# Three modulation panels of a gap at once, each in a column group of its own, with one set of transposes

## What is computed

```
mod  = jax.nn.silu(c)     @ w_ada[i] + b_ada[i]     # c, c_ctx: 1024 values; w_ada[i]: 1024 x 6144
modc = jax.nn.silu(c_ctx) @ w_ada[i] + b_ada[i]
sh1, sc1, gt1, sh2, sc2, gt2 = jnp.split(mod[:, None, :], 6, axis=-1)
h = rmsnorm(x, g_norm1[i]) * (1 + sc1) + sh1
```

## Time and profile before

| | us |
|---|---|
| median of 3 runs | 3118.34 (3117.12 to 3120.02) |
| the profiled execution | 3123.84 |
| its span in the trace | 3121.5 |
| TensorE busy | 2756.1 (88%) |
| TensorE weight loads busy | 1632.0 (52%) |
| VectorE busy | 811.8 (26%) |
| ScalarE busy | 506.5 (16%) |
| matmuls of the panels, line 538 | 384 records |
| matmuls of the folds, line 554 | 192 records |

### The profile page before, as it was taken

One profiled execution on the slowest core, in us unless ns is written; L12 is line 12 of the kernel. 1 busy time (PEld: TensorE's weight loads), 2 busy tenths in 40 slices (PEclk: granted clock), 3 DMA queues, 4 the chain that ended last, 5 costly groups with the idle time before them and its releaser, 6 DMA issues.

```text
span 3121.5 us, 30855 instructions
## 1 busy us (share of the span) xinstructions
PE 2756.1 (88%) x13271; PEld 1632.0 (52%) x13271; DVE 811.8 (26%) x1735; ACT 506.5 (16%) x1045; POOL 50.5 (2%) x76
## 2 busy tenths in 40 slices
PE   6989999999999999999997888988999996666766
PEld 4658887677885444444443323323456884222322
DVE  2343402153522534332212010111334412000001
ACT  1340001031002012122202111011211321000001
POOL 0000000000001100000000000000200000000000
PEclk8999999989999999999998999999999998777776
DMA  9346446417447311121213999999521334999996
GB/s 311 135 173 197 157 148 245 159 50 247 151 146 188 101 54 43 40 80 45 76 67 121 421 421 421 418 422 392 135 72 64 122 121 199 420 421 421 421 421 256
DMA packets 201225, 663.80 MB, mean 213 GB/s; under 512 B 13384, under 2 KB 59054, under 8 KB 151811
## 3 DMA queue, kind: packets, MB, share of 16 engines
q1 hardware_dynamic: 193987, 644.50, 54.0%
q0 software_dynamic: 7104, 17.34, 2.6%
HBM read 660.67 MB, written 9.57 MB: 215 GB/s over the span
## 4 chain that ended last, share of the span: by engine, by line
PE 71%; DMA 22%; DVE 3%; ACT 2%; issue 1%; SPq 0%; DVEq 0%; ACTq 0%
PE ps L447 38%; DMA ring<-in_w_e 22%; PE ps L468 7%; PE ps L948 6%; PE ps L579 5%; PE ps L494 2%; PE ps L538 1%; PE ps L903 1%; PE ps L769 1%; PE ps L747 1%; PE ps L929 1%; PE ps L758 1%; PE ps L554 1%; PE ps L801 1%; PE ps L823 1%
## 5 line engine op out<-in xcount | busy, mean ns | idle before, releaser
L447 PE MATMUL ps<-normed,ring 128*128 128x256 f32 (+1 forms) x3456 | 944.5, 434 | 30.9 <-issue 18.4
L948 PE MATMUL ps<-ring,arena 128*32 128x256 f32 (+1 forms) x4608 | 642.4, 540 | 211.7 <-DMA ring<-in_w_e 206.2
L447 PEld LDWEIGHTS ps<-normed,ring 128*128 128x128 f32 x3456 | 659.0, 192 | 294.7 <-issue 224.6
L948 PEld LDWEIGHTS ps<-ring,arena 128*32 128x32 f32 (+1 forms) x4608 | 204.9, 135 | 629.9 <-DMA ring<-in_w_e 329.4
L447 PE MATMUL ps<-arena,ring 128*128 128x256 f32 (+1 forms) x832 | 257.9, 468 | 6.6 <-DVE small L1071 6.6
L1136 DVE COPY arena<-ps 128x256 f32<-128x256 f32 (+1 forms) x152 | 79.9, 529 | 647.9 <-PE ps L447 315.9
L468 PE MATMUL ps<-ring,normed 128*128 128x512 f32 x512 | 222.0, 592 | 0.0
L447 PEld LDWEIGHTS ps<-arena,ring 128*128 128x128 f32 x832 | 158.6, 193 | 97.0 <-issue 75.5
L579 PE MATMUL ps<-arena,ring 128*128 128x256 f32 x704 | 156.8, 387 | 8.7 <-DVE arena L1185 8.7
L468 PEld LDWEIGHTS ps<-ring,normed 128*128 128x128 f32 x512 | 96.7, 190 | 117.3 <-issue 117.2
L579 PEld LDWEIGHTS ps<-arena,ring 128*128 128x128 f32 x704 | 136.7, 195 | 28.7 <-DVE arena L1185 9.4
(11 more groups left out here) (215 smaller groups left out, 1943.4 us busy)
## 6 DMA issues: line engine op xcount, KB each, us to landing
ring<-in_w_e SPq DMA_DIRECT2D x384, 1024.0 KB, 15.4
ring<-in_w_in SPq DMA_DIRECT2D x56, 1024.0 KB, 6.8
ring<-in_w_ada SPq DMA_DIRECT2D x48, 1024.0 KB, 7.3
ring<-in_ffn_w_up SPq DMA_DIRECT2D x88, 512.0 KB, 6.6
ring<-in_ffn_w_down SPq DMA_DIRECT2D x22, 1024.0 KB, 5.0
ring<-in_dil_w_qkv SPq DMA_DIRECT2D x18, 1024.0 KB, 7.3
ring<-in_sb_w_qkv SPq DMA_DIRECT2D x12, 1024.0 KB, 16.3
ring<-in_w_branch SPq DMA_DIRECT2D x12, 1024.0 KB, 7.4
```

The source lines that it names most:

```text
L447: ins = mm(o[:, 0:n], slots[k // 4][:, k % 4, f * P:(f + 1) * P], src[:, k, 0:n], start=k == 0, stop=k == kts - 1)
L948: ins = mm(o[w * g:w * g + w, 0:cols], lhs(2 * c + j), slot[:, j, g * cols:(g + 1) * cols], start=c == 0 and j == 0, stop=c == KT // 2 - 1 ...
```

## The change

A gap's three panels are computed together. Each panel gets a column group of its own (group 0, 1 or 2 of four) and sums over all eight slices in it, so PSUM holds complete sums and nothing has to be added up. The weight chunks of a gap come in another order: the first halves of the three panels, then the second halves. TensorE waits for three chunks, does the first four slices of all three panels, releases these three chunks with one `chunk_used`, waits for the next three and does the rest. ScalarE copies the 96 used partitions once. In place of three folds there is one set of four transposes (96 x 128 each), for all three panels, and it is called as a step of its own right behind the gap's matmuls. VectorE adds the bias once for all three panels. A gap takes two PSUM banks instead of six.

```diff
     def ada_gap(n):
-        for _ in range(n * ADA_GAP):
-            i, c0 = ada.pop(0)
-            panel(a["w_ada_2"][i], c0)
+        for _ in range(n):
+            panels = [ada.pop(0) for _ in range(ADA_GAP)]
+            for k0 in (0, 4 * P):
+                for i, c0 in panels:
+                    cols(a["w_ada_2"][i], k0, c0)
...
-            ada = {"part": 0, "fold": 0, "read": {}}
-
-            def ada_part():
-
-
-                slots = []
-                for slot, loaded, count in next_chunks(2):
-                    pe.wait_ge(loaded, count)
-                    slots.append(slot.rearrange("p (k n) -> p k n", k=4))
+            ada = {"gap": 0}
+
+            def ada_gap():
+
                 o = banks.open("a")
                 pe.wait_ge(*banks.due)
-                for k in range(KT):
-                    ins = mm(o[32 * (k % 4):32 * (k % 4) + 32, :], silu_pad[:, k, :], slots[k // 4][:, k % 4, :],
-                             start=k < 4, stop=k >= 4)
+                for k0 in (0, 4):
+                    slots = []
+                    for slot, loaded, count in next_chunks(ADA_GAP):
+                        pe.wait_ge(loaded, count)
+                        slots.append(slot.rearrange("p (k n) -> p k n", k=4))
+                    for k in range(4):
+                        for g, slot in enumerate(slots):
+                            ins = mm(o[32 * g:32 * g + 32, :], silu_pad[:, k0 + k, :], slot[:, k, :],
+                                     start=k0 + k == 0, stop=k0 + k == KT - 1)
+                    if k0 == 0:
+                        ins.then_inc(chunk_used, 1)
+                        used[0] += 1
+                        freed_at.extend([-used[0]] * ADA_GAP)
                 ins.then_inc(banks.filled, 1)
-                chunks_done(2)
-                ada["read"][ada["part"]] = sum(r[-1] == "a" for r in banks.uses)
-                ada["part"] += 1
+                chunks_done(ADA_GAP)
+                read = sum(r[-1] == "a" for r in banks.uses)
+                ada_turn.append((ada["gap"], read))
+                ada["gap"] += 1
+
+            ada_turn = []
 
             def ada_fold():
 
-                n = ada["fold"]
-                ada["fold"] += 1
-
-                pe.wait_ge(banks.freed["a"], ada["read"][n])
+                n, read = ada_turn.pop(0)
+                pe.wait_ge(banks.freed["a"], read)
                 o = banks.open("v")
                 pe.wait_ge(*banks.due)
                 for f in range(4):
-                    ins = mm(o[:, f * P:(f + 1) * P], ADA[n % 2][:, f * P:(f + 1) * P], cst("fold32"), start=True, stop=True)
+                    ins = nc.tensor.transpose(o[:, f * 96:(f + 1) * 96], ADA[n % 2][0:96, f * P:(f + 1) * P], ident[0:96, 0:96])
                 ins.then_inc(banks.filled, 1)
-
-            def ada_gap():
-                for n in range(ADA_GAP):
-                    ada_part()
-                    if n:
-                        ada_fold()
-                ada_fold()
...
                 mean_square(H, S, KT, mean)
                 ada_gap()
+                ada_fold()
...
             def ada_columns():
 
-                for _ in range(ADA_GAP):
-                    i, c = divmod(ada_done[0], N_MOD * D // BRANCH)
-                    ada_done[0] += 1
-                    o = banks.take("v")
-                    v.wait_ge(banks.filled, banks.at["v"])
-                    bada = b_ada[:, i * N_MOD * KT + 4 * c:i * N_MOD * KT + 4 * c + 4]
-                    ve.tensor_tensor(mods[i][:, 4 * c:4 * c + 4, :], o.rearrange("p (f s) -> p f s", s=P)[:, :, 0:2],
-                                     bada.unsqueeze(2).broadcast_to([P, 4, 2]), ALU.add
-                                     ).then_inc(banks.freed["v"], banks.free("v"))
+                i, c = divmod(ada_done[0], N_MOD * D // BRANCH)
+                ada_done[0] += ADA_GAP
+                o = banks.take("v")
+                v.wait_ge(banks.filled, banks.at["v"])
+                cols = o[:, 0:4 * 96].rearrange("p (f g s) -> p g f s", f=4, s=32)[:, :, :, 0:2]
+                f = slice(4 * c, 4 * (c + ADA_GAP))
+                bada = b_ada[:, i * N_MOD * KT:(i + 1) * N_MOD * KT][:, f].rearrange("p (g f) -> p g f", f=4)
+                ve.tensor_tensor(mods[i][:, f, :].rearrange("p (g f) s -> p g f s", f=4), cols,
+                                 bada.unsqueeze(3).broadcast_to([P, ADA_GAP, 4, 2]), ALU.add
+                                 ).then_inc(banks.freed["v"], banks.free("v"))
...
             def ada_copies():
-                for _ in range(ADA_GAP):
-                    o = banks.take("a")
-                    sc.wait_ge(banks.filled, banks.at["a"])
-                    se.activation(ADA[ada_copied[0] % 2], o, ACT.Copy).then_inc(banks.freed["a"], banks.free("a"))
-                    ada_copied[0] += 1
+                o = banks.take("a")
+                sc.wait_ge(banks.filled, banks.at["a"])
+                se.activation(ADA[ada_copied[0] % 2][0:96], o[0:96], ACT.Copy).then_inc(banks.freed["a"], banks.free("a"))
+                ada_copied[0] += 1
```

## The result

The changed kernel takes 3128.87 us, median of 13 runs (3126.7 to 3131.7), against 3120.02 us (3117.12 to 3129.43, 13 runs) for the kernel before: a ratio of 1.0024, 95% interval 1.0016 to 1.0033. It is slower, by 8.9 us in the medians; the forecast was 9.7. Run again on another chip it was 3129.65 against 3119.11, ratio 1.0035 (1.0023 to 1.0047).

A forecast was written before the change was run, and what follows sets the result against it. Weight transfers after the first slot release, not TensorE's work, were taken to end the pairs of gaps. Terms 5.2 + 4.4 - 1.7 + 1.4 + 0.4 = +9.7 us on 3118.3 gave 3128.0 us, range 3120 to 3136.

The forecast's parts named there:

- Release of the slots: In three pairs of gaps: first slots come free 1.72 us later, delaying weight loads and projection; +5.2 us, bounds 0 and 5.4.
- the chain a7 to f1 moves by 1.72: Weight loads from a pair's eighth chunk (a7) to the projection's second (f1) all shift 1.72 us, and the projection too.
- rival C: Weight transfers in the pairs catch up, each pair pays only 0.4 to 0.5 us: +3, 3121 us; chance 0.15.
- Clock in the second gap's wait: In each pair's second gap: one idle piece of about 5 us brings half clock; +4.4 us, bounds 0 and 7.5.
- Rival B: The clock does not fall in the pairs' new wait; only transfers count: +7.0 or 5.3 us, 3124.5; chance 0.22.
- The third pair's old half clock: Half clock of 3.4 us that the third pair had before should be replaced: -1.7 us, bounds -1.7 and 0.
- First gap: The projection's second chunk is issued later, beside dilated bias traffic, delaying the projection: +1.4 us.
- at most +1.7: Bound on the first gap's delay: the shift of its load's issue, from 31.4 to 33.1; at least 0.
- The gap's own length: Each gap on TensorE: 7.0 us matmuls, 0.88 bare wait, 0.6 transposes; 8.5 us against 8.4 before.
- rival D: Rounds of three matmuls set by weight loads, 0.33 us each; gaps 1.5 us shorter: 3109 us; chance 0.05.
- E: The three column groups do not overlap: 20.6 us of matmuls a gap, 13.6 more, eight times: 3227 us; chance 0.03.
- Last gap: Behind the last gap, ACT's squares start 0.5 us later, delaying mean square and norm: +0.4 us, bounds 0.1 and 0.6.

The follow-up runs named there:

- e1: Kernel before, a gap's first two chunks given back only with the second panel's: 3131.32 us against 3125.69, ratio 1.0017.
- e5: Kernel before, each chunk of a gap given back after its own four matmuls: 3120.26 us against 3119.11, ratio 0.9998.
- e2: Changed kernel with four dummy matmuls in the wait of each pair's second gap: 3130.05 us, ratio 1.0013 to the kernel before.
- e3: Changed kernel, the dilated bias table's large transfer issued only after the first projections: 3111.73 us, ratio 0.9955 to the kernel before.
- e9: Kernel before with 32 small dummy matmuls in the first gap, to move the instruction packets: 3124.34 us, ratio 1.0012.
- e10: Changed kernel with the late bias table transfer and a gap's matmuls ordered chunk by chunk: 3134.09 us, ratio 1.0028 to the kernel before.

## Why the prediction was right, and where by luck

**Release of the slots: right in kind, too large in size.** a7's issue moved by 1.7 us in every pair, and e1 and e5 show that the pair's end follows the release in both directions. But I put +1.72 on f1 in all three pairs, and the runs showed 1.8, 0.6 and 0.6. The step that failed is "the chain a7 to f1 moves by 1.72": it was rival C, the transfers that catch up, in two pairs of three, and by its own mechanism. The loss of 1.3 us that I saw between a7 and a11 did go into the idle time, because it came from an instruction packet whose place moved. 3.1 us in place of 5.2.

**Clock in the second gap's wait: right.** All three pairs have one idle piece (5.7, 4.3 and 4.3 us against my 5.4, 5.2 and 4.8) and half clock behind it. Expected +4.4, measured by e2 4.1. The second halves took 5.4, 6.4 and 6.2 us where e2 has 3.6, so 2.4 us a pair were lost in the mean (I had 2.2), and 1.0 of it was hidden (I had 0.75). TensorE and no longer f1 ends all three pairs, 0.6, 2.2 and 1.4 us behind f1's landing. Rival B is out. The third pair's old half clock went, -1.7 as put down, but that term was partly luck: of the seven traces without the change three have it behind that projection (240.3 to 240.7 us from there to the last gap), and four do not (238.5 to 239.1; after has 238.7).

**First gap: the term that was mis-sized.** I bounded it by the shift of the issue, 0 to 1.7, with 2 us of clock apart, and took +1.4; it was +4.1 (+5.5 in e1). The step that failed is "at most +1.7": I took the transfer's own time as fixed. The issue moved by 1.7 as reckoned, but the load then took 21.6 instead of 19.2 us (22.9 in e1), and e3 shows that it takes 5.1 without the table's transfer beside it. Why it took longer is open: it also took 21.5 and 22.2 us in e9 and e5 with no later release, so part of the 4.1 is that the trace of before had the shortest one. Against e9 the term is 1.8, close to the forecast.

**The gap's own length: right.** 7.07 us of matmuls (7.0), a bare wait of 0.70 (0.88) and 0.55 for the transposes (0.6): 8.4 us for 8.4. Rounds of three last 0.43, so rival D is out, and E with it. By the Trainium skill (TensorE: Matmul & The Clock Gate, What overlaps and what doesn't in The mechanism) matmuls are strict FIFO; e10's early start of the second panel beside the first one's fifth record disagrees.

**Last gap: right.** The rows that answer to the earlier trace rows:

```profile
984.58 0.59 ACT L1721 ACTIVATE arena<-ps 96x512 f32<-96x512 f32 x1 [4.81 <-PE ps L541]
985.08 3.88 ACT L1696 ACTIVATE normed<-residual 128x1024 f32<-128x1024 f32 x4
```

The squares start 7.62 us behind the gap's first matmul (977.46), before 7.14: +0.5, and PE waited 0.49 for them.

So the total of 9.7 against 8.9 is right partly by luck: the transfers gave back 2.1 us of the forecast, by a packet that happened to move, and in these two traces the first gap took 2.7 more.

## What to carry to other kernels

Where a phase waits for its weights, count from the first release of a slot, not from the work: a change that lets go of three slots at once, later, costs what it delays, and the arithmetic that it saves is worth nothing. Look also at what else is on the DMA engines when a load is moved, as one late load of 1 MB cost more in these two traces (4.1 us) than all three pairs' transfers (3.1), and moving the other transfer gained the kernel before 16 to 18 us in the medians on two chips. And look at what ends a phase before pricing the clock. One idle piece of 4.3 to 5.7 us brought half clock in every pair of after, and TensorE ended the pairs: 4.1 us. Waits of 2.4 us, with one of 1.6 or 2.1 us a little earlier, brought it in two of e1's three pairs, and f1 ended these pairs: nothing.

## What the runs showed of the hardware

One 16 KB packet of the instruction queue, about every 256 TensorE instructions, makes the 1 MB load under way land 0.6 to 1.5 us late. Column groups overlap out of program order, but only within a few records: 12.36 us for 48 records chunk by chunk, 7.07 in turn. Whether an idle time brings half clock can turn on its moment: TensorE waits 3.3 us in the second model in both kernels, and in the trace of before the clock is low from there on, in after not. In the kernel before:

```profile
1592.18 20.19 PE L447 MATMUL ps<-arena,ring 128*128 128x512 f32 x40 [3.30 <-DVE small L1071]
```

```profile
1590.90:1597.70 6.80, 5.52 (x7) 2.42 (x8) 1.19 (x2) 0.00 (x0) 0.00 (x0) 0.50 0.31 133
```

and in after:

```profile
1601.58 18.72 PE L449 MATMUL ps<-arena,ring 128*128 128x512 f32 x43 [3.29 <-DVE small L1078]
```

```profile
1600.00:1607.00 7.00, 5.42 (x13) 2.55 (x14) 1.49 (x2) 0.00 (x0) 0.00 (x0) 1.00 0.32 130
```

That alone is 2.8 us between two traces, and six of the thirteen traces lack it, with and without the change. It is the largest part of why the spans differ by 6.1 us where the stages say 9.9; that it is also part of why runs of one kernel spread over 12 us is likely but not shown.
